# Convolution taps of two tiles moved into the next tile, and the head norm by a square root and a reciprocal

## The chip, the cores and the metric

One NeuronCore of one Trainium2 chip runs the kernel. The metric is the device time of one execution in microseconds, the median of several runs; before the change it is 1832.07 us (three runs, 1827.65 to 1835.13). TensorE does the matmuls, VectorE and ScalarE the elementwise work, GpSimd and SyncE issue DMAs.

## The reference

A decoder layer on 256 tokens of width 2048, in float32. What matters here is the first half:

```python
proj = x @ w_in                      # K, V, Q of two head groups, gates, u, gate_b, gate_c
o_att = _nsa(q, k_cmp, v_cmp, ...)   # 8 heads of 128, three branches each, softmax
y = gate_b * conv3(gate_c * u)       # depthwise, causal, width 3, 1024 channels
def _head_rmsnorm(y, g):             # over each of the 16 groups of 128
    yf = yf * rsqrt(mean(square(yf), -1) + 1e-6)
    return yf * g
mix = _head_rmsnorm(concatenate([o_att, o_conv]), head_norm_g)
h = layernorm(ALPHA * x + mix @ w_out)
```

Behind it stands the second half: queries and top-k over product keys, then for each token 128 gathered rows of `expert_u` (a dot product and a gelu) and 128 of `expert_v` (a weighted sum), and a last layer norm.

## The kernel before, in words

Each engine has its own instruction stream, written out by hand; streams meet only in semaphores, so the order of the Python calls of an engine is the order of its queue.

**Items.** The input projection is 22 tiles of 256 output columns; tile `t` has 8 items `(t, c)`, each two blocks of 128 rows of the weight. The output projection follows with items `O(j, i)`, `j` 0 to 3 and `i` 0 to 15. Each item's weight block (128x512) is split in two parts for a float32-like product: ScalarE writes the high part (`hi_to`, L839), VectorE the rest (`lo_to`, L1130), and TensorE multiplies (12 matmuls of 256 columns at L512 for an input item, 6 of 512 at L652 for an output item). The ring of split blocks has six slots, so ScalarE can be at most six items ahead of TensorE. `hi_to(end)` and `lo_to(end)` make the items before `end`; a step written under `(t, c)` of ScalarE or VectorE stands behind the split of item `(t, c-1)`.

**Tiles.** The kinds of tiles 12 to 21 are K V Q Q C U B C U B, and tiles 2 to 11 have the same order. Heads of group 0 are worked through in tiles 10 to 15, of group 1 in 16 to 21: `score` on TensorE at c = 6 of one tile (L599 to L605), in the next tile `bias` (VectorE, c = 1), `expo` (ScalarE, c = 2 to 4), `scale` (VectorE, c = 4), `transpose_probs` (TensorE, c = 4, L613), `probs_out` (both, c = 7), `attend` (TensorE, c = 6, L633) and `att_out` (ScalarE, in the tile after).

**Convolution.** A C tile leaves its result in `c_sb`. Behind a U tile VectorE makes the product (`conv_in`, L1198) and three taps (`conv_tap`, L1207 and L1209), each of two instructions and a drain, behind a B tile the output product (`conv_out`, L1216). `cu` and `cv` have one buffer each.

**Head norm.** For a pair of blocks: `square` (ScalarE), `mean_square` (TensorE with a matrix of ones, L640), `log_rms` and `inverse_rms` (ScalarE, Ln then Exp with scale -0.5, L918 and L921), `normed` (VectorE, two products, L1225). Then `mix_att` and `mix_conv` (ScalarE) make the high part of the activations, `lo_att` and `lo_conv` (VectorE, L1230 and L1236) the low part; the output projection takes these. Group 0 goes through these steps in tiles 16 and 17, group 1 in tile 21 and the items `O(0, i)`. `score` of group 1's first head waits for `rms_ok` 4, since the mean squares lie in its PSUM banks.

Where the norm of the second group stands in ScalarE's queue:

```python
                if (t, c) == (21, 6):
                    log_rms(0, 5)
                    log_rms(2, 6)
                if (t, c) == (21, 7):
                    log_rms(1, 7)
                    act.drain()
        hi_to(O(0, 0))
        inverse_rms(0)
        inverse_rms(2)
```

Of the kernel before, what the change touches and what calls it, by code (L numbers as in the profile page):

```python
# [14 lines left out]
SEQ = 256  # L15
# [59 lines left out]
def O(j, i):  # L75
    return ITEM["O", j, i]
# [18 lines left out]
def evicted(t):  # L95
    act_tiles = [i for i in range(TILES) if kind_of(i) in "KVQC"]
    dve_tiles = [i for i in range(TILES) if kind_of(i) in "cUB"]
    return ("acc_act", act_tiles.index(t) + 1) if t in act_tiles else ("acc_dve", dve_tiles.index(t) + 1)


def build(nc, x, w_in, cmp_k_pos, cmp_k_w1, cmp_k_b1, cmp_k_w2, cmp_v_pos, cmp_v_w1, cmp_v_b1, cmp_v_w2,
# [184 lines left out]
    def bview(i, *shape):  # L286
        n = 1
        for s in shape:
            n *= s
        names_ = "abc"[:len(shape)]  # L290
        if len(shape) == 1:
            return bank[i][:, 0:n]
        return bank[i][:, 0:n].rearrange("p (%s) -> p %s" % (" ".join(names_), " ".join(names_)),
                                         **dict(zip(names_, shape)))
# [196 lines left out]
    def _(pe):  # L491
# [177 lines left out]
        for t in range(2, TILES):  # L669
            sem, count = evicted(t - 2)  # L670
            pe.wait_ge(S[sem], count)
            for c in range(8):
                if t < 10:
                    c_slot(8 * (t - 2) + c)
                if (t, c) == (3, 4):
                    gate_logits()
                if (t, c) == (4, 4):
                    gate_transposes()
                if (t, c) == (6, 2):
                    hid_sum(0)  # L680
                if (t, c) == (10, 1):
                    hid_sum(1)
                if (t, c) == (10, 3):
                    hid_transposes()
                if (t, c) == (10, 5):
                    compressed()
                for g in range(NG):
                    r = t - 10 - 6 * g
                    if c == 4 and 1 <= r <= R:
                        transpose_probs(g, r - 1)  # L690
                    if c == 6 and 1 <= r <= R:
                        attend(g, r - 1)
                    if c == 6 and 0 <= r < R:
                        score(g, r)
                if (t, c) == (15, 6):
                    for n, ready in ((2, 1), (3, 2), (0, 3), (1, 4)):
                        mean_square(n, ready)
                if (t, c) == (21, 4):
                    mean_square(0, 5)
                    mean_square(2, 6)  # L700
                if (t, c) == (21, 5):
                    mean_square(1, 7)
                t_slot(t, c)

        for j in range(4):
            if j == 0:
                pe.wait_ge(S["y_att"], R * NG)
                pe.wait_ge(S["mix_ready"], 1)
            elif j == 1:
                for t in (20, 21):  # L710
                    pe.wait_ge(S[evicted(t)[0]], evicted(t)[1])
            else:
                pe.wait_ge(S["acc_dve"], 2 + 4 * NG + j - 1)
            if j == 3:
                pe.wait_ge(S["s_skeys"], 16)
                for n in range(4):
                    for i in range(4):
                        ins = nc.tensor.transpose(bank[2 + n][:, 128 * i:128 * i + 128], skeys[:, 4 * n + i, :], ident[:, :])
                    ins.then_inc(S["sk_mm"], 1)
            for i in range(KC):  # L720
                if (j, i) == (0, 5):
                    mean_square(3, 8)
                if (j, i) == (0, 8):
                    pe.wait_ge(S["mix_ready"], 2)
                if (j, i) == (0, 14):
                    pe.wait_ge(S["mix_ready"], 3)
                out_item(j, i)
# [92 lines left out]
    def _(act):  # L820
# [92 lines left out]
            nc.scalar.activation(sq[:, 2 * n:2 * n + 2, :], y_sb[:, 2 * n:2 * n + 2, :], ACT.Square  # L913
                                 ).then_inc(S["squared"], 1)

        def log_rms(n, count):
            act.wait_ge(S["norm_mm"], count)
            nc.scalar.activation(sq[:, 2 * n:2 * n + 2, :], bview(2 + n, 2, SEQ), ACT.Ln, bias=eps[:, 0:1])  # L918

        def inverse_rms(n):  # L920
            nc.scalar.activation(sq[:, 2 * n:2 * n + 2, :], sq[:, 2 * n:2 * n + 2, :], ACT.Exp, scale=-0.5  # L921
                                 ).then_inc(S["rms_ok"], 1)

        def mix_att(g):
# [19 lines left out]
        for t in range(2, TILES):  # L944
            for c in range(8):
# [30 lines left out]
                    square(0, 0)  # L976
                if (t, c) == (15, 2):
                    square(1, 0)
                if (t, c) == (16, 1):
                    log_rms(2, 1)  # L980
                    log_rms(3, 2)
                if (t, c) == (16, 2):
                    log_rms(0, 3)
                    log_rms(1, 4)
                    act.drain()
                if (t, c) == (16, 3):
                    for n in (2, 3):
                        inverse_rms(n)
                if (t, c) == (16, 4):
                    for n in (0, 1):  # L990
                        inverse_rms(n)
                if (t, c) == (16, 7):
                    mix_conv(0, 0, 4, 1)
                if (t, c) == (17, 0):
                    mix_att(0)
                if (t, c) == (20, 0):
                    square(0, 0)
# [1 line left out]
                    square(2, 3)  # L999
                if (t, c) == (21, 2):  # L1000
                    square(1, 0)
                if (t, c) == (21, 6):
                    log_rms(0, 5)
                    log_rms(2, 6)
                if (t, c) == (21, 7):
                    log_rms(1, 7)
                    act.drain()
        hi_to(O(0, 0))
        inverse_rms(0)
        inverse_rms(2)  # L1010
        hi_to(O(0, 1))
        inverse_rms(1)
        hi_to(O(0, 3))
        mix_att(1)
        hi_to(O(0, 4))
        mix_conv(1, 0, 2, 2)
        hi_to(O(0, 5))
        square(3, 4)
        hi_to(O(0, 9))
        log_rms(3, 8)  # L1020
        act.drain()
        hi_to(O(0, 10))
        inverse_rms(3)
        hi_to(O(0, 11))
        mix_conv(1, 2, 4, 3)
        for n in range(4):
            hi_to(O(3, 4 + n))
# [92 lines left out]
    def _(dve):  # L1120
# [80 lines left out]

        def conv_tap(t, tap):
            g, pair = (t - 2) // 10, (t - 2) % 10 // 8
            for b in range(2):
                w = params[:, 8 * tap + R * g + 2 * pair + b:8 * tap + R * g + 2 * pair + b + 1]
                if tap == 0:
                    V.tensor_scalar(cv[:, b, :], cu[:, b, 0:SEQ], w, None, ALU.mult)  # L1207
                else:
                    V.scalar_tensor_tensor(cv[:, b, :], cu[:, b, tap:tap + SEQ], w, cv[:, b, :], ALU.mult, ALU.add)  # L1209
            dve.drain()  # L1210
# [9 lines left out]
        def normed(g, n, count):  # L1220

            dve.wait_ge(S["rms_ok"], count)
            for b in range(2 * n, 2 * n + 2):
                col = 24 + NH * (b // 4) + R * g + b % 4
                V.scalar_tensor_tensor(y_sb[:, b, :], y_sb[:, b, :], params[:, col:col + 1], sq[:, b, :],  # L1225
                                       ALU.mult, ALU.mult)
# [43 lines left out]
        for t in range(2, TILES):  # L1270
            for c in range(8):
                lo_to(T(t, c))
                first = 2 if t < 10 else 5
                if t > 2 and c == first and kind_of(t - 1) == "U":
                    conv_in(t - 1)
                    conv_tap(t - 1, 0)
                if t > 2 and c == first + 1 and kind_of(t - 1) == "U":
                    conv_tap(t - 1, 1)
                if t > 2 and c == first + 2 and kind_of(t - 1) == "U":
                    conv_tap(t - 1, 2)  # L1280
                if t > 2 and c == first and kind_of(t - 1) == "B":
                    conv_out(t - 1)
                if (t, c) == (4, 6):
# [20 lines left out]
                for g in range(NG):  # L1304
# [4 lines left out]
                        scale(g, r)  # L1309
                    if 0 <= r < R and c == 7:  # L1310
                        probs_out(g, r)
                if (t, c) == (16, 4):
                    normed(0, 2, 1)
                if (t, c) == (16, 5):
                    normed(0, 3, 2)
                    dve.drain()
                if (t, c) == (16, 6):
                    normed(0, 0, 3)
                if (t, c) == (16, 7):
                    normed(0, 1, 4)  # L1320
                    dve.drain().then_inc(S["mixf_ready"], 1)
                if (t, c) == (17, 0):
                    lo_conv(0, 0, 4, 1)
                if (t, c) == (17, 3):
                    lo_att(0, 2)
                    dve.drain().then_inc(S["mix_ready"], 1)
        lo_to(O(0, 2))
        normed(1, 0, 5)
        normed(1, 2, 6)
        lo_to(O(0, 3))  # L1330
        normed(1, 1, 7)
        dve.drain().then_inc(S["mixf_ready"], 1)
        lo_to(O(0, 5))
        conv_out(21)
        lo_to(O(0, 6))
        lo_att(1, 3)
        lo_conv(1, 0, 2, 4)
        dve.drain().then_inc(S["mix_ready"], 1)
        lo_to(O(0, 10))
        normed(1, 3, 8)  # L1340
        dve.drain().then_inc(S["mixf_ready"], 1)
        lo_to(O(0, 12))
        lo_conv(1, 2, 4, 5)
        dve.drain().then_inc(S["mix_ready"], 1)
        for j in range(3):
# [197 lines left out]
```

## Time and profile before

| | |
|---|---|
| median of three runs | 1832.07 us (1827.65 to 1835.13) |
| the profiled execution | 1834.16 us, its span 1832.4 us |
| mean granted TensorE clock | 0.961 |
| TensorE busy | 1492.4 us, 81% of the span |
| VectorE busy | 1062.5 us, 58% |
| GpSimd busy | 754.5 us, 41% |
| ScalarE busy | 393.9 us, 21% |
| input and output projection | end at about 464 us |
| first expert gather | issued at 493.8 us |

The span is what lies between the first and the last instruction that the profile shows; the profiled execution's time is 1.8 us more. The busy shares are means over two stages: in the projections TensorE works almost without a pause, in the gathers the DMA engines do (421 GB/s from about 600 us on). A row of a timeline reads: start in us, duration in us, engine, line, instruction, output<-inputs, shape and count; in brackets stands the idle time of the engine ahead of it and what ended it.

### The profile page before, as it was taken

Reading aid. Unit: us, or ns where it says so; the run is one execution under the profiler, and the core shown is the slowest. Engines: PE = TensorE matmul, PEld = TensorE weight load, DVE = VectorE, ACT = ScalarE, POOL = GpSimd, SP = SyncE. Lnnn points to the kernel's source line nnn. Section 1 sums busy time; section 2 is a strip of 40 time slices with the busy share of each in tenths; the row PEclk is TensorE's granted clock in tenths of the full one; section 3 lists DMA queues with packets and bytes.
Section 4 is the critical chain, followed back from the end, with each engine's and each line's share of the span. In section 5 each row is a group of like instructions: output and inputs, shape, how many; then the busy total and the mean of one; then the engine's idle time right before and its main releaser. Section 6 shows DMA issues by size and latency. Waiting matters only on the chain.

```text
span 1832.4 us, 15277 instructions
## 1 busy us (share of the span) xinstructions
PE 1492.4 (81%) x5692; PEld 885.1 (48%) x5692; DVE 1062.5 (58%) x1696; ACT 393.9 (21%) x853; POOL 754.5 (41%) x591
## 2 busy tenths in 40 slices
PE   8999999999887428787787877777778788787896
PEld 7988998978876323333333333333333333233332
DVE  6665656565679997454545545454746454544434
ACT  5665464565101030101001011010110201010200
POOL 3210000000157768555455454555555555455341
PEclk9999999999998668999999999999999999999998
DMA  9885344376499999999999999999999999999995
GB/s 305 286 264 157 110 139 137 116 234 202 168 408 414 413 378 422 422 421 421 422 421 422 421 422 422 421 422 421 422 422 422 421 422 421 422 422 421 422 421 222
DMA packets 154043, 644.60 MB, mean 352 GB/s; under 512 B 11620, under 2 KB 64960, under 8 KB 87920
## 3 DMA queue, kind: packets, MB, share of 16 engines
q0 software_dynamic: 79376, 557.62, 74.0%
q1 hardware_dynamic: 74592, 85.99, 14.8%
q8 instruction: 45, 0.74, 0.2%
q14 instruction: 30, 0.25, 0.0%
HBM read 641.47 MB, written 2.10 MB: 351 GB/s over the span
## 4 chain that ended last, share of the span: by engine, by line
DMA 52%; PE 31%; POOL 6%; DVE 6%; issue 3%; DVEq 1%; ACT 1%; SPq 0%; POOLq 0%; ACTq 0%
DMA v_slot<-in_expert_v_dram,eid 50%; PE psum_all L512 12%; PE psum_all L813 7%; PE psum_all L652 4%; POOL u_slot L461 4%; DVE u_slot L1453 3%; PE psum_all L751 2%; POOL v_slot L476 2%; DMA u_slot<-in_expert_u_dram,eid 2%; PE psum_all L633 1%; PE psum_all L539 1%; PE psum_all L537 1%; DVE w_lo L1130 1%; PE psum_all L599 0%; ACT w_hi L839 0%
## 5 line engine op out<-in xcount | busy, mean ns | idle before, releaser
L813 PE MATMUL psum_all<-v_slot,diag 128*128 128x512 f32 x1968 | 906.0, 608 | 248.6 <-DMA v_slot<-in_expert_v_dram,eid 248.5
L1453 DVE SCALAR_TENSOR_TENSOR u_slot<-u_slot,xh 128x2048 f32<-128x2048 f32 x256 | 581.8, 2290 | 493.5 <-DMA u_slot<-in_expert_u_dram,eid 493.2
L813 PEld LDWEIGHTS psum_all<-v_slot,diag 128*128 128x128 f32 x1968 | 360.9, 191 | 793.1 <-issue 436.2
L476 POOL DMA_INDIRECT v_slot<-in_expert_v_dram,eid x256 | 349.4, 1365 | 463.5 <-PE psum_all L813 434.8
L461 POOL DMA_INDIRECT u_slot<-in_expert_u_dram,eid x256 | 367.8, 1437 | 219.6 <-DVE eid L1446 94.2
L1067 ACT ACTIVATE diag<-ident,gate 128x128 f32<-128x128 f32 x246 | 73.5, 388 | 710.7 <-PE psum_all L813 465.4
L1130 DVE TENSOR_TENSOR w_lo<-w_ring,w_hi 128x512 fp32r<-128x512 f32 x240 | 156.8, 687 | 87.9 <-ACT w_hi L839 85.0
L512 PE MATMUL psum_all<-act_hi,w_hi 128*128 128x256 f32 x640 | 186.5, 291 | 1.1 <-DVE w_lo L1130 1.0
L512 PE MATMUL psum_all<-act_hi,w_lo 128*128 128x256 f32 x640 | 181.8, 284 | 0.0
L512 PE MATMUL psum_all<-act_lo,w_hi 128*128 128x256 f32 x640 | 181.8, 284 | 0.0
L839 ACT ACTIVATE w_hi<-w_ring 128x512 fp32r<-128x512 f32 x240 | 139.3, 622 | 42.4 <-PE psum_all L512 40.6
L751 PE MATMUL psum_all<-hT,wq_ring 128*128 128x256 f32 (+1 forms) x576 | 122.1, 374 | 21.3 <-DMA wq_ring<-in_w_query_dram 20.8
L512 PEld LDWEIGHTS psum_all<-act_hi,w_hi 128*128 128x128 f32 x640 | 123.5, 193 | 13.6 <-issue 4.3
L512 PEld LDWEIGHTS psum_all<-act_lo,w_hi 128*128 128x128 f32 x640 | 123.3, 193 | 3.1 <-issue 0.7
L512 PEld LDWEIGHTS psum_all<-act_hi,w_lo 128*128 128x128 f32 x640 | 123.3, 193 | 0.0
L751 PEld LDWEIGHTS psum_all<-hT,wq_ring 128*128 128x128 f32 x576 | 104.7, 201 | 35.8 <-DMA wq_ring<-in_w_query_dram 22.3
L449 POOL DMA_DIRECT2D skeys<-in_sub_keys_dram x1 | 1.2, 1177 | 252.8 <-PE psum_all L652 252.8
L1058 ACT ACTIVATE u_act<-u_dot 128x16 f32<-128x16 f32 x16 | 3.4, 215 | 318.4 <-DVE u_slot L1453 318.4
L1130 DVE TENSOR_TENSOR w_lo<-wq_ring,w_hi 128x512 fp32r<-128x512 f32 x64 | 42.7, 690 | 28.0 <-ACT w_hi L839 27.7
L652 PE MATMUL psum_all<-w_hi,mix_hi 128*128 128x512 f32 x128 | 50.4, 394 | 3.5 <-DVE w_lo L1130 3.5
L1491 DVE SCALAR_TENSOR_TENSOR xh<-v_slot,gate,xh 128x2048 f32<-128x2048 f32 x10 | 23.5, 2351 | 51.0 <-DMA v_slot<-in_expert_v_dram,eid 51.0
L652 PE MATMUL psum_all<-w_hi,mix_lo 128*128 128x512 f32 x128 | 49.8, 389 | 0.0
(226 smaller groups left out, 1005.5 us busy)
## 6 DMA issues: line engine op xcount, KB each, us to landing
w_ring<-in_w_in_dram SPq DMA_DIRECT2D x88, 512.0 KB, 5.2
wq_ring<-in_w_out_dram SPq DMA_DIRECT2D x32, 512.0 KB, 5.0
wq_ring<-in_w_query_dram SPq DMA_DIRECT2D x32, 512.0 KB, 10.5
w_ring<-in_cmp_k_w_dram POOLq DMA_DIRECT2D x16, 512.0 KB, 6.5
w_ring<-in_cmp_v_w_dram POOLq DMA_DIRECT2D x16, 512.0 KB, 4.6
u_slot<-in_expert_u_dram,eid POOLq DMA_INDIRECT x256, 32.8
v_slot<-in_expert_v_dram,eid POOLq DMA_INDIRECT x256, 33.2
xh<-in_x_dram SPq DMA_DIRECT2D x4, 512.0 KB, 7.6
```

The source lines that it names most:

```text
L461: nc.gpsimd.indirect_dma_start(out=u_slot[m % RU][:, :], out_offset=None, in_=expert_u[0], in_offset=bass.IndirectOffsetOnAxis(ap=eid[:, n ...
L476: nc.gpsimd.indirect_dma_start(out=v_slot[m % RV][:, :], out_offset=None, in_=expert_v[0], in_offset=bass.IndirectOffsetOnAxis(ap=eid[:, n ...
L512: ins = nc.tensor.matmul(o, st, mv, start=(k == 0 and b == 0 and i == 0), stop=(k == KC - 1 and i == 2), skip_group_check=True)
L537: nc.tensor.matmul(acc[0:62, :], blk_hl[:, kv, j, 0:62], w_hi[:, n % RING, :], start=(j == 0), stop=False, skip_group_check=True)
L652: ins = nc.tensor.matmul(bank[acc + b][:, :], st[:, k, half], mv[:, n % RING, :], start=(i == 0 and m == 0), stop=(i == KC - 1 and m == 2))
L751: ins = nc.tensor.matmul(o, wq_ring[j % 2][:, k // 4, k % 4, 256 * (h % 2) + 128 * c:256 * (h % 2) + 128 * c + 128], hT[:, k, 128 * t0:128 ...
L813: ins = nc.tensor.matmul(bank[(4 if n < PH else 0) + q][:, :], diag[:, n % 2, k, :], v_slot[m % RV][:, 512 * q:512 * q + 512], start=m % ( ...
L839: nc.scalar.activation(w_hi[:, n % RING, :], raw_item(n), ACT.Copy).then_inc(S["hi_done"], 1)
L1067: ins = nc.scalar.activation(diag[:, n % 2, k, :], ident[:, :], ACT.Copy, scale=gate[:, n, k:k + 1])
L1130: V.tensor_tensor(w_lo[:, n % RING, :], raw_item(n), w_hi[:, n % RING, :].bitcast(F32), ALU.subtract).then_inc(S["lo_done"], 1)
L1453: V.scalar_tensor_tensor(u_slot[m % RU][:, :], u_slot[m % RU][:, :], 1.0, xh[:, n // PH, :], ALU.mult, ALU.mult, accum_out=u_dot[:, n, k:k ...
L1491: V.scalar_tensor_tensor(xh[:, 1, :], v_slot[m % RV][:, :], gate[:, n, k:k + 1], xh[:, 1, :], ALU.mult, ALU.add)
```

## The change

Three taps of tile 10 move from tile 11 (c = 5, 6, 7) to tile 12 (c = 0, 2, 3), those of tile 17 from tile 18 to tile 19 likewise; tiles 7 and 20 keep theirs. The root of the mean square is taken by Sqrt on ScalarE in one pass, its reciprocal on VectorE in `normed`, in place, with a drain. In tile 16 ScalarE has one root behind each of four items and VectorE one norm behind each of four; the steps that follow move by one to three items. In the second group no root is left in tile 21: the first three lie behind `O(0, 0)` and `O(0, 1)`, the mean squares all at (21, 5), the fourth ahead of `O(0, 7)` in place of `O(0, 5)`.

```diff
+TAP_AT = {7: ((8, 2), (8, 3), (8, 4)), 10: ((12, 0), (12, 2), (12, 3)), 17: ((19, 0), (19, 2), (19, 3)),
+          20: ((21, 5), (21, 6), (21, 7))}
...
-                if (t, c) == (21, 4):
+                if (t, c) == (21, 5):
                     mean_square(0, 5)
                     mean_square(2, 6)
-                if (t, c) == (21, 5):
                     mean_square(1, 7)
...
-                if (j, i) == (0, 5):
+                if (j, i) == (0, 7):
                     mean_square(3, 8)
...
-        def log_rms(n, count):
+        def root_rms(n, count):
             act.wait_ge(S["norm_mm"], count)
-            nc.scalar.activation(sq[:, 2 * n:2 * n + 2, :], bview(2 + n, 2, SEQ), ACT.Ln, bias=eps[:, 0:1])
-
-        def inverse_rms(n):
-            nc.scalar.activation(sq[:, 2 * n:2 * n + 2, :], sq[:, 2 * n:2 * n + 2, :], ACT.Exp, scale=-0.5
+            nc.scalar.activation(sq[:, 2 * n:2 * n + 2, :], bview(2 + n, 2, SEQ), ACT.Sqrt, bias=eps[:, 0:1]
                                  ).then_inc(S["rms_ok"], 1)
...
-                if (t, c) == (16, 1):
-                    log_rms(2, 1)
-                    log_rms(3, 2)
-                if (t, c) == (16, 2):
-                    log_rms(0, 3)
-                    log_rms(1, 4)
-                    act.drain()
-                if (t, c) == (16, 3):
-                    for n in (2, 3):
-                        inverse_rms(n)
-                if (t, c) == (16, 4):
-                    for n in (0, 1):
-                        inverse_rms(n)
-                if (t, c) == (16, 7):
+                if t == 16 and 1 <= c <= 4:
+                    root_rms((2, 3, 0, 1)[c - 1], c)
+                if (t, c) == (17, 0):
                     mix_conv(0, 0, 4, 1)
-                if (t, c) == (17, 0):
+                if (t, c) == (17, 1):
                     mix_att(0)
...
-                if (t, c) == (21, 6):
-                    log_rms(0, 5)
-                    log_rms(2, 6)
-                if (t, c) == (21, 7):
-                    log_rms(1, 7)
-                    act.drain()
-        hi_to(O(0, 0))
-        inverse_rms(0)
-        inverse_rms(2)
         hi_to(O(0, 1))
-        inverse_rms(1)
-        hi_to(O(0, 3))
+        root_rms(0, 5)
+        root_rms(2, 6)
+        hi_to(O(0, 2))
+        root_rms(1, 7)
+        hi_to(O(0, 6))
         mix_att(1)
-        hi_to(O(0, 4))
         mix_conv(1, 0, 2, 2)
-        hi_to(O(0, 5))
+        hi_to(O(0, 7))
         square(3, 4)
-        hi_to(O(0, 9))
-        log_rms(3, 8)
-        act.drain()
         hi_to(O(0, 10))
-        inverse_rms(3)
-        hi_to(O(0, 11))
+        root_rms(3, 8)
+        hi_to(O(0, 12))
         mix_conv(1, 2, 4, 3)
...
             g, pair = (t - 2) // 10, (t - 2) % 10 // 8
+            if tap == 0 and t in (10, 17):
+                dve.drain()
...
             dve.wait_ge(S["rms_ok"], count)
+            V.reciprocal(sq[:, 2 * n:2 * n + 2, :], sq[:, 2 * n:2 * n + 2, :])
+            dve.drain()
...
-                    conv_tap(t - 1, 0)
-                if t > 2 and c == first + 1 and kind_of(t - 1) == "U":
-                    conv_tap(t - 1, 1)
-                if t > 2 and c == first + 2 and kind_of(t - 1) == "U":
-                    conv_tap(t - 1, 2)
+                for u in (7, 10, 17, 20):
+                    for tap in range(3):
+                        if (t, c) == TAP_AT[u][tap]:
+                            conv_tap(u, tap)
...
-                if (t, c) == (16, 4):
-                    normed(0, 2, 1)
-                if (t, c) == (16, 5):
-                    normed(0, 3, 2)
-                    dve.drain()
-                if (t, c) == (16, 6):
-                    normed(0, 0, 3)
+                if t == 16 and 4 <= c <= 7:
+                    normed(0, (2, 3, 0, 1)[c - 4], c - 3)
                 if (t, c) == (16, 7):
-                    normed(0, 1, 4)
                     dve.drain().then_inc(S["mixf_ready"], 1)
-                if (t, c) == (17, 0):
+                if (t, c) == (17, 3):
                     lo_conv(0, 0, 4, 1)
-                if (t, c) == (17, 3):
+                if (t, c) == (17, 5):
                     lo_att(0, 2)
                     dve.drain().then_inc(S["mix_ready"], 1)
         lo_to(O(0, 2))
         normed(1, 0, 5)
+        lo_to(O(0, 3))
         normed(1, 2, 6)
-        lo_to(O(0, 3))
+        lo_to(O(0, 4))
         normed(1, 1, 7)
         dve.drain().then_inc(S["mixf_ready"], 1)
         lo_to(O(0, 5))
         conv_out(21)
-        lo_to(O(0, 6))
+        lo_to(O(0, 7))
         lo_att(1, 3)
+        lo_to(O(0, 8))
         lo_conv(1, 0, 2, 4)
         dve.drain().then_inc(S["mix_ready"], 1)
-        lo_to(O(0, 10))
+        lo_to(O(0, 11))
         normed(1, 3, 8)
         dve.drain().then_inc(S["mixf_ready"], 1)
-        lo_to(O(0, 12))
+        lo_to(O(0, 13))
         lo_conv(1, 2, 4, 5)
```

## Rows read from the trace of the kernel before

**Rows 1.** The page: the chain that ended last, by engine.
```profile
DMA 52%; PE 31%; POOL 6%; DVE 6%; issue 3%; DVEq 1%; ACT 1%; SPq 0%; POOLq 0%; ACTq 0%
```

**Rows 2.** Waits of TensorE, 0 to 430 us: total, times, longest.
```profile
PE psum_all L652 <- DVE w_lo L1130: 3.5, 4, 1.5
PE psum_all L633 <- DVE pTc L1191: 1.6, 1, 1.6
PE psum_all L633 <- issue: 1.5, 1, 1.5
```

**Rows 3.** VectorE's timeline, from 180 us.
```profile
182.97 0.75 DVE L1160 SCALAR_TENSOR_TENSOR sc<-dist,nslope,psum_all 128x512 f32<-128x512 f32 x1 [1.59 <-PE psum_all L605]
...
188.69 0.69 DVE L1130 TENSOR_TENSOR w_lo<-w_ring,w_hi 128x512 fp32r<-128x512 f32 x1 [0.60 <-ACT w_hi L839]
...
190.81 0.18 DVE L1184 TENSOR_TENSOR scc<-scc,rg 128x30 f32<-128x30 f32 x1
...
191.51 0.68 DVE L1198 TENSOR_TENSOR cu<-psum_all,c_sb 128x512 f32<-128x512 f32 x1
...
196.43 0.40 DVE L1191 COPY pTc<-psum_all 16x256 f32<-16x256 f32 x1
```

**Rows 4.** The chain that ended last, in order of time: start, duration, what.
```profile
196.98 3.51 PE psum_all L633 x16
...
204.01 9.31 PE psum_all L512 x72
...
233.76 2.36 PE psum_all L633 x16
...
237.98 8.73 PE psum_all L512 x72
...
250.46 2.36 PE psum_all L633 x16
...
313.28 3.73 PE psum_all L633 x16
...
320.53 9.11 PE psum_all L512 x72
...
361.27 1.72 PE psum_all L640 x4
...
383.08 57.42 PE psum_all L652 x252
```

**Rows 5.** A stretch of 4 us: busy times, granted clock, DMA share, GB/s.
```profile
198.00:202.00 4.00, 4.00 (x15) 3.28 (x15) 0.03 (x1) 0.90 (x2) 0.00 (x0) 0.55 0.89 238
```

**Rows 6.** Groups of VectorE instructions by form: busy, mean ns, idle before.
```profile
L1130 DVE TENSOR_TENSOR w_lo<-w_ring,w_hi 128x512 fp32r<-128x512 f32 x240 | 156.8, 687 | 87.9 <-ACT w_hi L839 85.0 <-issue 0.8
...
L1225 DVE SCALAR_TENSOR_TENSOR y_sb<-y_sb,params,sq 128x256 f32<-128x256 f32 x16 | 6.9, 480 | 1.2 <-ACT sq L921 1.2
...
L1459 DVE RECIPROCAL g_inv<-g_sum 128x1 f32<-128x1 f32 x16 | 2.5, 157 | 0.0
...
L1177 DVE RECIPROCAL rg<-sums 128x6 f32<-128x6 f32 x8 | 1.5, 183 | 0.0
...
L1180 DVE TENSOR_TENSOR rg<-rg,gates 128x6 f32<-128x6 f32 x8 | 1.3, 166 | 0.6
```

**Rows 7.** ScalarE's timeline, 255 to 365 us.
```profile
260.96 1.28 ACT L918 ACT_TABLE_LOAD   x1
265.43 0.69 ACT L918 ACTIVATE sq<-psum_all,eps 128x512 f32<-128x512 f32 x1 [3.18 <-PE psum_all L640]
...
285.18 0.51 ACT L884 ACTIVATE sc<-sc,nmx 128x256 f32<-128x256 f32 x1 [3.14 <-DVE nmx L1172]
...
362.17 0.69 ACT L918 ACTIVATE sq<-psum_all,eps 128x512 f32<-128x512 f32 x1 [4.69 <-PE psum_all L640]
```

**Rows 8.** TensorE's timeline, 276 to 292 us.
```profile
279.32 1.03 PE L599 MATMUL psum_all<-kT,qT 128*128 128x256 f32 x4
...
289.51 0.39 PE L512 MATMUL psum_all<-act_hi,w_hi 128*128 128x256 f32 x1 [0.26 <-DVE w_lo L1130]
```

## The prediction

> **What bounds the kernel now.** Read first the chain that ended last [rows 1]: DMA holds 52% of it and TensorE 31%. The DMA share is the expert gathers, which begin only after the input projection, the output projection, the layer norm and the first query scores. So the span is a TensorE stage of 464 us followed by gathers, and whatever the first stage saves reaches the end one for one, as long as nothing between waits for something other than the work before it; I found nothing of that kind. The change edits only the first stage, between 190 and 390 us.
>
> The waits of TensorE come next [rows 2]. It is busy nearly everywhere there: it waits 1.6 us once and 1.5 us once at L633 (the attention products of a head), and 3.5 us in four pieces at L652 (the output projection). These small waits are the prize, and with them what the clock does after them. The chain in order of time [rows 4] shows that. An undisturbed head starts L633 at 233.76 and its tile goes on at 237.98, 4.22 us later, and the next 72 matmuls take 8.73. After the first wait it is 196.98 to 204.01, 7.03 us, and then 9.31; after the second 313.28 to 320.53, 7.25, and then 9.11. In those microseconds the granted clock is 0.55 [rows 5], the lower of its levels (1.2 of 2.4 GHz) for most of the slice. TensorE had worked without a pause for 12 us before, then stood 1.6 us, then fell. So each wait costs itself and a second bill: 2.81 + 0.58 = 3.39 us for the first, 3.03 + 0.38 = 3.41 for the second.
>
> **Part A, the taps of tiles 10 and 17.** In the VectorE timeline [rows 3] the scaled probabilities of head 0 are out at 190.99. A split item, the gating product (191.51, 0.68), and then tap, item, tap, item, tap stand before the two copies that L633 waits for, which end at 196.83; L633 starts at 196.98, 1.6 us late. Moving the three taps takes them from between. The items stay: the product ends at 192.2, two items of 0.65 (0.687 long, but 0.62 apart in a row) [rows 6] bring 193.5, and the transposes are done by about 192.6, so the copies end at about 194.25. L633 can start when TensorE comes to it, at 196.98 - 1.6 = 195.4: a margin of 1.1 us. The same holds for tile 17.
>
> Where do the taps go? The first lands behind the copies, where VectorE stands idle until the next head's scores. The others go behind the second and third item of the next tile. Call S the moment a head's scores are out; in rows 3 that is 182.97, and the probabilities are out at S + 8.0. TensorE transposes them at S + 8.73 [rows 4] and comes to the next L633 at 250.46 - 237.98 = S + 12.48. In the wait for exponentials VectorE idles ahead of each of those items, 0.60 us ahead of the one at 188.69 and more ahead of the one before; a tap is 2 x 0.48 with some overlap, 0.87, plus a drain of 0.07. The second tap fits; the third overruns its gap by about 0.3. So the probabilities are out at S + 8.3 against S + 8.73, and the copies at about S + 11.85 against S + 12.48. Both margins hold, the smaller is 0.4. Part A gives 1.6 + 3.39 + 1.5 + 3.41 = **9.9 us**. Its bounds: 3.1, if the clock falls anyway, and 9.9, if not; I take 9.9, because the heads of rows 4 without a wait ran at full clock.
>
> **Part B, the norm of the first group (tile 16).** Removed on ScalarE: four Exp passes, and the table load between Ln and Exp. The Ln pass becomes a Sqrt of the same shape; I cost it like Ln, 0.69 [rows 7]. Added on VectorE: four reciprocals of 128x512 and four drains. Its price is the unknown. At small sizes the trace has it [rows 6]: 157 ns for one element, 183 for six, while an ordinary product of six takes 166. One of 512 takes about 0.69, a slope of (687 - 166) / 506 = 1.03 ns per element. The reciprocal's own slope from one to six is 26 / 5 = 5.2 ns, which drawn out to 512 would be 2.8 us; but most of it is the step that small operations show among themselves, and beside the product of six only 17 ns are left. So it lies between 0.53 (the slope alone) and 2.8, and I take 0.69, since it is nearest to the product.
>
> The first mean square is out at 265.4 [rows 7]. ScalarE runs Sqrt, item, Sqrt, item and is through the four at 269.4. VectorE finishes the third item at 269.5, and each norm is 0.69 + 0.07 + 0.88 and an item 0.65, 2.3 us: the norm of the four is complete at about 278.0. TensorE needs items (16,4) to (16,6) at 276.4, 277.9 and 281.2; they are there at 271.8, 274.1 and 276.4. Scores start at 279.32 [rows 8] and are out at S = 279.32 + (4.22 - 2.36) = 281.2. Before, the subtraction for the low parts of the convolution stands ahead of the head's bias. Now both subtractions are moved behind the third and fifth item, so the bias starts at S. The probabilities come at S + 8.5, TensorE is there at S + 8.73; the copies at S + 12.4 against S + 12.48. Nothing has room to spare, so I charge 0.3. Before, item (17,3) started at 289.51 where S + 5 x 1.455 = 288.45, 1.06 late, and there was some 0.3 more up to the head: 1.4. Part B gives 1.4 - 0.3 = **1.1 us**, with 0.69 for the reciprocal.
>
> A table load for Exp now stands ahead of the head's exponentials. ScalarE idled 3.14 us there [rows 7], by my times 2.8 after the change. In the trace a load runs ahead of the wait of its pass (Ln's in tile 16 ends 3.18 us before the pass can start, the idle time of that row), so its 1.28 are covered; without cover it would cost 1.3 once. The Trainium skill (ScalarE: Activation LUTs, "Table sets: the hidden batching unit" and "What ACT_TABLE_LOAD costs") speaks against mixing Exp and Sqrt, since they lie in different sets, and gives 2.66 us for a switch with its drain; the trace has 1.28 and starts the pass right behind. By the page's figure the load would still lie inside the idle time, by 0.1 us, and the sum would be the same.
>
> **Part C, the norm of the second group (tile 21 and the output projection).** From 361.27 to 383.08 [rows 4] TensorE does four mean squares (0.86 each), four items of tile 21 (1.455) and six of the projection (6 x 0.228 = 1.37): 3.44 + 5.82 + 8.2 = 17.46 of 21.81 us. So 4.35 us are lost. The reason is on ScalarE [rows 7]: it stands 4.69 us at the first Ln, with items (21,6) and (21,7) behind it in its queue, and VectorE stands behind those; then come two more Exp loads. After the change no norm step lies in tile 21. ScalarE makes (21,6), (21,7) and O(0,0) as slots come free, to 360.3, loads Sqrt while it waits, and is through three roots at 366.3. VectorE does tap 1 at about 359 as before, then (21,6), tap 2, (21,7), O(0,0) to 362.3, O(0,1) at 366.4, and norm, item, norm, item, norm to 372.5. TensorE wants O(0,0) at 369.6 and then one item each 1.37: O(0,2) at 372.4 (there at 368.7), O(0,3) at 373.7 (370.9), O(0,4) at 375.1 (373.2), O(0,5) at 376.4 (374.7), O(0,6) at 377.8 (375.4). The fourth mean square is moved behind that, its square is ready at 375.3; its root, norm and subtraction end at 386.2 and are wanted at 389.6. I find no wait left. Part C gives **4.3 us**; bounds: 4.35, all that is lost, and 2, taken lower than that delay would give, if the chain of norms on VectorE runs two microseconds later than I count, a little more than its least margin (1.7 at O(0,5)). The weight loads that the earlier splits release start earlier, on the one sync queue, and nothing waits on it here.
>
> Sum: 9.9 + 1.1 + 4.3 = 15.3 us, from 1834.16 of the profiled execution to 1818.9. That execution is 2.1 above the median, so in terms of the median 1832.07 - 15.3 = **1817**.
>
> **The rivals.**
> 1. The clock falls anyway, or one of the two waits stays (the taps' new places push the next head's copies past their 0.4 to 0.6 of margin). Two short waits gone without their clock give 3.1 + 1.1 + 4.3 = 8.5 us, 1823.5; one wait of two kept 15.3 - 4.9 = 10.4, 1821.7. Against it: three heads in a row without a wait and at full clock. Chance 0.13.
> 2. The reciprocal is dear, at the bound of 2.8 us. Each norm in tile 16 is 3.8, item (16,7) is out at 287.2 and the bias starts at 288.9, 7.7 behind S: 6.3 us lost against before (7.7 less the 1.4 lost there now), 9.7 if the clock falls there. In the projection O(0,3) and O(0,4) wait 1.6 and 3.1 and a later item 1.0, 1.5 us worse than before. Together -9.9 + 6.3 + 1.5 = -2.1, or +1.3: 1830 to 1833, no change. Chance 0.06.
> 3. The other side: the reciprocal works eight steps for each element, 8 x 1.03 x 512 = 4.2 us. Then the bias behind tile 16 starts at 295, 13.7 behind S (12.3 us lost against before, and 3.4 of clock) and the projection loses 7.3: -9.9 + 15.7 + 7.3 = +13, 1845. It ends slower by over 0.5% from about 3.9 us on. Six elements would then hold 49 of the 183 ns and one would take 142, not 157; that speaks against it. The Trainium skill (VectorE: DVE Perf Modes, "First, the fixed hardware budget") says the reciprocal is an iterative divide with a repeat count of 8, which could be read this way. Chance 0.04.
> 4. The saving is real but smaller, by new waits of 0.5 to 1 us in tile 17 or in O(0,2) to O(0,6), or is hidden by the scatter of the gathers (the three runs before span 7.5 us): 1820 to 1827. Chance 0.12.
>
> **How the numbers follow.** The forecast has 0.65, with 1813 to 1821 as its own range (Part C at 2 to 4.35, Part B at 0 to 1.4, scatter of 3). The range that leaves out 2 in 10 takes in rival 1 and most of 4: 1812 to 1825. About 0.5% (9 us, 1823) can be told from no change here. Faster: the forecast, half of rivals 1 and 4, 0.77; same: 0.18, with rival 2; slower: 0.05.
>
> **What would show it.** Part A: no idle time at L633 in tiles 11 and 18, and a granted clock of 1.00 where it was 0.55. Part B: RECIPROCAL 128x512 at about 0.69 us; the load of Exp ahead of the exponentials of tile 17 ended before them; L633 of tile 17 without a wait. Part C: O(0,0) to O(0,6) back to back, ScalarE's first root after O(0,0)'s split. The prediction is wrong if the reciprocal is over 1.5 us, if a new wait ahead of an L633 brings the clock down, or if the gathers' stage, 464 us to the end, changes its length.

## The result and the profile after

| | before | after |
|---|---|---|
| median | 1832.11 us (14 runs, 1826.39 to 1836.81) | 1838.28 us (14 runs, 1836.12 to 1839.22) |
| profiled execution | 1834.16, span 1832.4 | 1838.75, span 1836.8 |
| ratio, with 95% interval | | 1.0034 [1.0023, 1.0045] |

The kernel became 0.34% slower where 0.8% faster was forecast; the time lies 13 us above the upper end of the range. By the bound set in the prediction (0.5%) this is "no change", but the interval lies wholly above 1: the loss is small and real.

The first view to open is the one that the prediction staked itself on, VectorE's groups by form in the changed kernel (busy, mean ns of one, idle before):

```profile
L1204 DVE RECIPROCAL sq<-sq 128x512 f32<-128x512 f32 x8 | 26.8, 3346 | 0.0
L1437 DVE RECIPROCAL g_inv<-g_sum 128x1 f32<-128x1 f32 x16 | 2.5, 158 | 0.0
L1156 DVE RECIPROCAL rg<-sums 128x6 f32<-128x6 f32 x8 | 1.5, 184 | 0.0
```

A reciprocal of 128x512 takes 3.35 us, not 0.69. The short ones are as short as before [rows 6].

The waits of TensorE up to 430 us (total, times, longest) answer to [rows 2]:

```profile
PE psum_all L656 <- DVE w_lo L1109: 7.3, 3, 3.3
...
PE psum_all L516 <- DVE w_lo L1109: 6.6, 5, 3.1
```

Both waits at the attention products (now L637) are gone. In their place TensorE waits 6.6 us for splits of the input projection, in pieces of up to 3.1 and all but 0.5 of it in tiles 16 and 17, and 7.3 in the output projection, in pieces of up to 3.3. What holds the splits is plain in VectorE's timeline, tile 16 first, then the second group:

```profile
264.04 0.69 DVE L1109 TENSOR_TENSOR w_lo<-w_ring,w_hi 128x512 fp32r<-128x512 f32 x1 [0.41 <-ACT w_hi L842]
264.65 3.35 DVE L1204 RECIPROCAL sq<-sq 128x512 f32<-128x512 f32 x1
268.07 0.88 DVE L1208 SCALAR_TENSOR_TENSOR y_sb<-y_sb,params,sq 128x256 f32<-128x256 f32 x2
268.87 0.68 DVE L1109 TENSOR_TENSOR w_lo<-w_ring,w_hi 128x512 fp32r<-128x512 f32 x1
269.47 3.35 DVE L1204 RECIPROCAL sq<-sq 128x512 f32<-128x512 f32 x1
...
373.98 0.68 DVE L1109 TENSOR_TENSOR w_lo<-wq_ring,w_hi 128x512 fp32r<-128x512 f32 x1
374.58 3.35 DVE L1204 RECIPROCAL sq<-sq 128x512 f32<-128x512 f32 x1
378.00 0.88 DVE L1208 SCALAR_TENSOR_TENSOR y_sb<-y_sb,params,sq 128x256 f32<-128x256 f32 x2
379.00 0.69 DVE L1109 TENSOR_TENSOR w_lo<-wq_ring,w_hi 128x512 fp32r<-128x512 f32 x1
```

From 264.04 on each split comes 4.8 us after the last, while TensorE eats an item in 1.45. ScalarE's timeline shows the same from its side: it has filled the ring and stands until the norms are through, and the load of Exp has little idle time left to hide in:

```profile
283.48 1.06 ACT L930 ACTIVATE mix_hi<-y_sb 128x1024 fp32r<-128x1024 f32 x1 [13.91 <-DVEq L1297]
...
286.54 1.28 ACT L887 ACT_TABLE_LOAD   x1
288.45 0.51 ACT L887 ACTIVATE sc<-sc,nmx 128x256 f32<-128x256 f32 x1 [0.62 <-DVE nmx L1151]
...
378.95 1.06 ACT L926 ACTIVATE mix_hi<-y_sb 128x1024 fp32r<-128x1024 f32 x1 [10.06 <-DVEq L1309]
```

Windows of 4 us (busy time of PE, PEld, DVE, ACT, POOL; then granted clock, DMA share, GB/s) show the clock. The stretch of [rows 5] is now at 1.00, and the fall has moved to where the new waits are:

```profile
198.00:202.00 4.00, 4.00 (x32) 3.90 (x33) 2.11 (x5) 0.86 (x2) 0.00 (x0) 1.00 0.55 142
...
280.00:284.00 4.00, 1.15 (x8) 0.85 (x7) 3.81 (x4) 0.52 (x1) 0.00 (x0) 0.57 0.00 0
...
376.00:380.00 4.00, 0.72 (x3) 0.25 (x2) 3.81 (x5) 1.05 (x2) 0.00 (x0) 0.52 0.84 260
```

The chain in order of time (start, duration, what) gives the balance. These rows answer to [rows 4]:

```profile
195.56 2.36 PE psum_all L637 x16
...
199.78 8.73 PE psum_all L516 x72
...
259.72 0.87 PE psum_all L644 x2
...
294.28 0.56 PE psum_all L617 x4
...
361.34 1.73 PE psum_all L644 x4
...
393.56 50.62 PE psum_all L656 x222
...
467.76 0.69 DVE xh L1228
```

The last row starts where the output projection ends. The same marks in the trace of before are 264.53 (mean squares), 291.21 (transposes of tile 17), 361.27 (mean squares, one item of 1.455 us earlier in the order) and 464.07. So by stretches: to the mean squares 264.53 - 259.72 = 4.8 us gained (first taps); to tile 17, 34.56 against 26.68, 7.9 lost (norm of the first group); to tile 21, 65.6 against 70.1, 4.5 gained (second taps); to the end, 107.9 against 102.8, 5.1 lost (norm of the second group). Together 3.7 us lost, 467.76 - 464.07. The gathers' stage is 0.7 us longer in this trace than in that of before (1365.1 against 1364.4), so the spans differ by 4.4. The medians differ by 6.2; the section on why the prediction was wrong tells where the rest is.

### The profile page after: what moved, and what is told of

It reads as the page before. It is cut to its first block, busy times and chain, and to the rows that moved or that the text cites. A ratio compares the mean times of both kernels' runs of the same rounds, so it can differ in the third digit from the quotient of the medians.

```text
span 1836.8 us, 15279 instructions
## 1 busy us (share of the span) xinstructions
PE 1492.0 (81%) x5692; PEld 883.5 (48%) x5692; DVE 1088.9 (59%) x1704; ACT 384.2 (21%) x841; POOL 754.6 (41%) x591
## 4 chain that ended last, share of the span: by engine, by line
DMA 53%; PE 31%; DVE 6%; POOL 5%; issue 2%; DVEq 1%; ACT 1%; SPq 0%; POOLq 0%
DMA v_slot<-in_expert_v_dram,eid 50%; PE psum_all L516 13%; PE psum_all L816 7%; PE psum_all L656 4%; POOL u_slot L465 4%; DVE u_slot L1431 3%; PE psum_all L754 2%; DMA u_slot<-in_expert_u_dram,eid 2%; POOL v_slot L480 1%; PE psum_all L637 1%; DVE sq L1204 1%; PE psum_all L543 1%; PE psum_all L541 1%; DVEq L1205 1%; DVE w_lo L1109 1%
## 6 DMA issues: line engine op xcount, KB each, us to landing
wq_ring<-in_w_query_dram SPq DMA_DIRECT2D x32, 512.0 KB, 18.8
```

## The experiments

The kernel before was run again beside each set of experiments, and its medians differ between the three sets: 1832.1 beside the changed kernel, 1827.9 beside experiments 1 to 4, 1833.8 beside 5 to 7. A ratio is always to the runs of before in the same set, and each experiment is also read by its own trace. Experiments 3 and 5 leave the reciprocal out of some norms, so their results are wrong and only their times are used.

**1. The taps alone.** Edit: the diff's lines of `TAP_AT`, the drain and the loop over it, on the kernel before.

```diff
+TAP_AT = {7: ((8, 2), (8, 3), (8, 4)), 10: ((12, 0), (12, 2), (12, 3)), 17: ((19, 0), (19, 2), (19, 3)),
...
+                        if (t, c) == TAP_AT[u][tap]:
+                            conv_tap(u, tap)
```

> The kernel before with the three taps of tiles 10 and 17 moved and nothing else. Theory (each short wait at the attention products costs itself and 3.4 us at the lower clock, and the moved taps end both): 9.9 us faster than before, no idle time of TensorE at that line, granted clock 1.00 behind it. Rival (the clock falls there whatever stands before it): 3.1 us faster.

Measured: 1825.52 us (12 runs, 1823.81 to 1826.6), ratio 0.9978 [0.9966, 0.9989], so 4 us by the ratio, 2.4 by the medians. The waits at the attention products are gone and the clock is 1.00 behind them:

```profile
198.00:202.00 4.00, 4.00 (x33) 3.92 (x32) 2.31 (x6) 0.66 (x2) 0.00 (x0) 1.00 0.47 119
```

Its trace reaches the first normalised `xh` at 458.07 us against 467.98 in the profiled execution of before: 9.9 us, the forecast to the tenth. Its median gives less than half. Neither theory as written fits both. The two numbers look to be about different executions of the kernel before; experiments 2 and 6 bear on this.

**2. The norm alone.** Edit: the changed kernel with the taps back, and without the drain that went with them.

```diff
-TAP_AT = {7: ((8, 2), (8, 3), (8, 4)), 10: ((12, 0), (12, 2), (12, 3)), 17: ((19, 0), (19, 2), (19, 3)),
+TAP_AT = {7: ((8, 2), (8, 3), (8, 4)), 10: ((11, 5), (11, 6), (11, 7)), 17: ((18, 5), (18, 6), (18, 7)),
...
-            if tap == 0 and t in (10, 17):
-                dve.drain()
```

> The changed kernel with the taps back in their old places, so the norm part alone. Theory (two parts of opposite sign: the taps give 9.9 us, the norm with its dear reciprocal takes them and some 6 more): about 16 us slower than before, 0.9%. Rival (the taps gave little, the norm costs only what is seen): 6 us slower.

Measured: 1844.16 us (6 runs), ratio 1.0074 [1.0052, 1.0096]; 16.3 us by the medians, 13.5 by the ratio. So the norm part alone loses 13 to 16 us, as the first theory has it, and the taps take some of it back. The front stage of its trace is only 9.8 us longer than that of before (first normalised `xh` at 477.73 against 467.98), and the trace shows why. Both waits at the attention products are there, 1.6 and 1.5 us long, yet only the first is followed by a fall of the clock. The chain in tile 18, behind the second wait:

```profile
321.21 2.60 PE psum_all L637 x16
...
325.67 8.74 PE psum_all L516 x72
```

and the windows of the stretch behind each wait:

```profile
320.00:324.00 4.00, 2.79 (x17) 2.34 (x18) 2.24 (x5) 0.15 (x1) 0.00 (x0) 1.00 0.27 62
...
200.00:204.00 4.00, 4.00 (x15) 3.42 (x15) 0.00 (x0) 0.90 (x2) 0.00 (x0) 0.50 0.60 156
```

From 321.21 to 325.67 are 4.46 us, where an undisturbed head has 4.22. In the trace of before the same wait of 1.5 us at the same place is followed by 7.25 us. The same wait has two prices, some 0.2 and 3.4 us. The norm's 7.9 + 5.1 = 13.0 us, less one fall of 3.4 that did not come, are 9.6, near the 9.8 of the trace.

**3. A product in the reciprocal's place.** Edit, on the changed kernel:

```diff
-            V.reciprocal(sq[:, 2 * n:2 * n + 2, :], sq[:, 2 * n:2 * n + 2, :])
+            V.tensor_tensor(sq[:, 2 * n:2 * n + 2, :], sq[:, 2 * n:2 * n + 2, :], sq[:, 2 * n:2 * n + 2, :], ALU.mult)
```

> The changed kernel, all steps in the same places, but each of the eight reciprocals of 128x512 is a product of the same size (so the norm uses the square of the root, not its reciprocal). Theory (the only step of the prediction that failed is the duration of the reciprocal, 0.69 taken and 3.35 measured): the product takes 0.69 us and the kernel 15 us less than before, about 1817. Rival (the Sqrt pass, the load of Exp ahead of tile 17 or the new order cost as well): no faster than about 1825.

Measured: 1818.85 us (6 runs), ratio 0.9941 [0.9919, 0.9962]; the eight products take 0.684 us each. No wait for a split is left in tiles 16 and 17 or in the projection, and the chain runs through both groups:

```profile
288.47 2.36 PE psum_all L637 x16
...
351.40 2.57 PE psum_all L644 x6
...
358.28 9.55 PE psum_all L656 x42
...
368.70 55.80 PE psum_all L656 x246
```

The x42 are seven output items back to back, the mean square of the fourth pair, then the rest without a gap. The projection ends at 448.06, 16.0 us before that of before (464.07). This is the kernel that the prediction reckoned with, at 1834.16 - 15.3 = 1818.9. By the stretches used above, the trace gains 5.5 us up to the mean squares and 4.5 from tile 17 to tile 21 (Part A: 9.9 forecast), 1.35 from the mean squares to tile 17 (Part B: 1.1) and 4.7 behind (Part C: 4.3). With the reciprocal at a product's price, every term comes out within 0.4 us. That the median meets 1818.9 so closely is in part luck: the profiled execution of this kernel took 1817.84.

**4. The disputed cost by itself.** Edit, on the changed kernel behind VectorE's last step:

```diff
+        for m in (1, 2, 4, 8, 16, 32, 64, 128, 256, 512):
+            dve.drain()
+            V.reciprocal(u_slot[0][:, 0:m], ln2g_sb[:, 0:m])
+            dve.drain()
+            V.tensor_tensor(u_slot[1][:, 0:m], ln2g_sb[:, 0:m], ln2g_sb[:, 0:m], ALU.mult)
```

> The changed kernel with pairs of a reciprocal and a product of 1, 2, 4, ... 512 columns behind its last step on VectorE. Theory A (a constant price for each column, (3346 - 184) / 506 = 6.25 ns, from the first column on): 128x64 takes about 0.55 us, 128x256 about 1.75, and between 1 and 8 columns the growth is 44 ns. Theory B (short ones run at the pace of a product and a slower pace sets in with size): 128x16 and 128x32 within 20 ns of the product. The same reciprocal on 32 partitions tells whether the partitions matter: 3.35 us if not.

The kernel was run once (1853.23 us, with the added work at its end), and only the durations in its trace are used. VectorE's timeline behind the last step:

```profile
1834.85 0.16 DVE L1498 RECIPROCAL u_slot<-ln2g_sb 128x1 f32<-128x1 f32 x1
...
1836.28 0.20 DVE L1498 RECIPROCAL u_slot<-ln2g_sb 128x8 f32<-128x8 f32 x1
1836.56 0.17 DVE L1500 TENSOR_TENSOR u_slot<-ln2g_sb 128x8 f32<-128x8 f32 x1
...
1837.37 0.35 DVE L1498 RECIPROCAL u_slot<-ln2g_sb 128x32 f32<-128x32 f32 x1
1837.80 0.19 DVE L1500 TENSOR_TENSOR u_slot<-ln2g_sb 128x32 f32<-128x32 f32 x1
...
1838.07 0.55 DVE L1498 RECIPROCAL u_slot<-ln2g_sb 128x64 f32<-128x64 f32 x1
...
1840.39 1.75 DVE L1498 RECIPROCAL u_slot<-ln2g_sb 128x256 f32<-128x256 f32 x1
...
1842.71 3.35 DVE L1498 RECIPROCAL u_slot<-ln2g_sb 128x512 f32<-128x512 f32 x1
1846.14 0.69 DVE L1500 TENSOR_TENSOR u_slot<-ln2g_sb 128x512 f32<-128x512 f32 x1
1846.90 3.34 DVE L1502 RECIPROCAL u_slot<-ln2g_sb 32x512 f32<-32x512 f32 x1
```

Theory A holds from the first columns on: (3.35 - 0.55) / 448 = 6.25 ns per column, against (0.69 - 0.19) / 480 = 1.04 for the product, six times as much. A quarter of the partitions takes as long (3.34 us). At 128x32 the two are already 0.16 us apart, which rules out theory B.

**5. Where the reciprocals hurt.** Edit, on the changed kernel:

```diff
+            if g == 0:
+                V.reciprocal(sq[:, 2 * n:2 * n + 2, :], sq[:, 2 * n:2 * n + 2, :])
+            else:
+                V.tensor_tensor(sq[:, 2 * n:2 * n + 2, :], sq[:, 2 * n:2 * n + 2, :], sq[:, 2 * n:2 * n + 2, :], ALU.mult)
```

> The changed kernel with its reciprocals in the first group's norm alone and a product of the same size in the second. From the two traces the first group's reciprocals cost 7.9 + 1.1 = 9.0 us against the product and the second group's 5.1 + 4.3 = 9.4. Theory (two separate costs that add): about 9 us above the kernel with the product in both, so 1828. Rival (the second is late because the first was): less than 4 us below the changed kernel.

Measured: 1828.40 us (12 runs, 1827.62 to 1829.09), 9.6 above the kernel with eight products and 9.9 below the changed kernel. The rival, which had less than 4 us below the changed kernel, is out. The trace says the same by stretches: from the mean squares to tile 17 it has 34.55 us, as the changed kernel (34.56; 25.33 with eight products), and from tile 21 to the end 98.1, as with eight products (98.1; 107.9 in the changed kernel). So the two costs, 9.2 and 9.8 us, are separate and add.

**6. The clock behind a wait.** Edit, on the kernel before: the three taps of tiles 10 and 17 are done twice, so that each of the two waits is longer.

```diff
                     conv_tap(t - 1, 2)
+                    if t in (11, 18):
+                        for tap in range(3):
+                            conv_tap(t - 1, tap)
```

> The kernel before, but the three taps of tiles 10 and 17 are done twice in a row (same result), so that each of the two waits at the attention products is some 2.6 us longer. Theory (after a wait of 1.6 us the clock falls in some executions and not in others, which is why the runs of before lie in three heaps, near 1827.5, 1831.5 and 1835; after one of 4 us it falls in every one): one heap, near 1827.5 + 5.2 + 6.8 = 1839.5, with a span of the runs under 4 us. Rival (the heaps come from the gathers): the same three heaps, each 5.2 us or more higher.

Measured: 1841.59 us (6 runs, 1840.40 to 1843.12), one heap with a span of 2.7 us, and 2.1 us above the 1839.5 expected. The waits are 4.2 and 4.1 us, and the clock falls with both (granted 0.50 at 200 to 204 us and at 320 to 324). The chain:

```profile
199.01 4.64 PE psum_all L633 x16
...
207.18 8.80 PE psum_all L512 x72
...
318.57 4.64 PE psum_all L633 x16
...
326.73 8.76 PE psum_all L512 x72
```

From 199.01 to 207.18 it is 8.17 us against 4.22. The 16 products take 4.64 us, about twice the 2.36 of an undisturbed head (3.51 in [rows 4]), so they run at the lower clock nearly from the first on, and a fall costs 4.0 us in place of 3.4. The lowest heap plus 2 x 2.6 plus 2 x 4.0 is 1840.7, near what was measured.

The 48 runs of before lie at 1825.6 to 1828.8 (20 runs), 1830.8 to 1832.4 (12) and 1833.8 to 1836.8 (16). The middles of these heaps, 1827.6, 1831.6 and 1835.2, are 3.7 to 4.0 us apart, about a fall each. Their mix differs between the sets, which is why the medians do: 4, 6 and 4 runs beside the changed kernel, 12, 2 and 3 beside experiments 1 to 4, and 4, 4 and 9 beside 5 to 7. That the heaps are executions with no, one and two falls is inferred, not shown: there is one trace of the kernel before, from the top heap, and it has both falls. Three things speak for it. The same wait has two prices in experiment 2. The mean granted clock, recorded for 34 of these runs, is 0.968 in the lowest heap, 0.964 in the middle one and 0.963 in the top one; it sets the lowest apart and hardly parts the other two. And the rival, that the heaps come from the gathers, has the traces against it: from the first normalised `xh` to the end of the span it is 1832.4 - 467.98 = 1364.4 us before, 1365.1 after, 1365.2 with the taps alone, 1364.7 with the norm alone and 1364.6 here, a spread smaller than the gap between two heaps. Since they are single traces of different kernels, they do not exclude it.

**7. Ln and Exp in the new places.** The changed kernel, its steps set apart as in the change, but without the reciprocal:

```diff
+        def inverse_rms(n):
+            nc.scalar.activation(sq[:, 2 * n:2 * n + 2, :], sq[:, 2 * n:2 * n + 2, :], ACT.Exp, scale=-0.5
+                                 ).then_inc(S["rms_ok"], 1)
...
+                if (t, c) == (16, 5):
+                    act.drain()
+                    inverse_rms(2)
+                    inverse_rms(3)
+                if (t, c) == (16, 6):
+                    inverse_rms(0)
+                    inverse_rms(1)
...
         root_rms(1, 7)
+        act.drain()
+        for n in (0, 2, 1):
+            inverse_rms(n)
...
         hi_to(O(0, 12))
+        act.drain()
+        inverse_rms(3)
...
-            V.reciprocal(sq[:, 2 * n:2 * n + 2, :], sq[:, 2 * n:2 * n + 2, :])
-            dve.drain()
```

(`root_rms` does Ln here; VectorE does two norms at (16, 6) and two at (16, 7).)

> The changed kernel (taps moved, the norm's steps and the steps behind it in the new places) with Ln and Exp on ScalarE in place of Sqrt and reciprocal: in tile 16 one Ln behind each of four items, two Exp at (16,5) and two at (16,6), in the second group the Exp passes behind the third Ln and, for the last pair, behind O(0,11). Theory (only the reciprocal's 3.35 us hurt; ScalarE has the room): no wait left but at most 1 us in the projection, front stage within 1 us of that with the product, so 1818 to 1821, faster than both kernels. Rival (the table loads between Ln and Exp hold the splits again): 1822 or more.

Measured: 1819.34 us (6 runs, 1818.71 to 1821.08), ratio 0.9934 [0.9914, 0.9954], within the 1818 to 1821 expected. It beats both kernels, with the four Exp passes of each group and the table loads kept. TensorE waits nowhere between its first input and the layer norm for more than 0.5 us:

```profile
PE psum_all L742 <- DVE xh L1372: 4.9, 1, 4.9
...
PE psum_all L516 <- DVE w_lo L1124: 0.5, 1, 0.5
```

So the new order was what paid. The Exp passes and loads that the change removed cost next to nothing once the steps stand apart: only for the fourth pair of the second group do a load (369.69, 1.28 us) and an Exp pass stand in the chain, and there TensorE is held up by some 0.2 us.

## Why the prediction was wrong, point by point

**The step that failed** is in Part B: "So it lies between 0.53 (the slope alone) and 2.8, and I take 0.69, since it is nearest to the product." It measured 3.35, above the upper bound. So the norm of the first group, for which Part B forecast a gain of 1.1 us, lost 7.9, and that of the second, for which Part C forecast a gain of 4.3, lost 5.1. The rows gave the slope, 26 / 5 = 5.2 ns for a column, and experiment 4 measured 6.25. I argued this slope away as a step that small operations share, by comparing a reciprocal and a product of six columns, where 17 ns of difference seemed little. By experiment 4 the reciprocal costs 6.25 - 1.04 = 5.2 ns a column more than the product, 31 ns on six columns, and the fixed parts of the two need not be equal. Where a slope of the operation itself is in the trace, it outweighs a likeness to another operation. The bound of 2.8 was that slope drawn out over 511 columns plus the 157 ns of the first, and left the slope no error. It was short by 1.05 ns on each column, 0.54 us in all. A slope taken from five columns and two different lines is too rough for that, and its end should not have been a wall.

**The rivals** had it between them. Rival 2 (2.8 us) said -2.1 or +1.3, rival 3 (4.2 us) +13; at 3.35 it was +4.6 by the profiled executions (1838.75 - 1834.16). Interpolated between +1.3 and +13 that would be 6, so the mechanism of both, norms that hold splits until TensorE starves and its clock falls, was the right one, and its price nearly so. They had 0.10 of the chance. The rule of the Trainium skill named beside rival 3 (VectorE: DVE Perf Modes, "First, the fixed hardware budget": an iterative divide with a repeat count of 8) did point to the side that came true; the trace's price is 6.25 / 1.04, six of a product's columns and not eight. I gave it 0.04 because "one would take 142, not 157". That speaks against eight steps and not against six: at 6.25 ns a column the 183 ns of six columns put one column at 152. I weighed 2.8 and 4.2 and no price between them.

**Part A** (9.9 us): near the forecast in the traces (4.8 and 4.5 in the changed kernel, 9.9 in the taps alone). The margins held: the new head in tile 19 was late by 0.2 us, that of tile 12 not at all. But 9.9 was read from a profiled execution in which the clock fell behind both waits. If the heaps are what experiment 6 takes them for, it fell about once in a median execution beside the changed kernel, so the taps are worth 6.5 there, and 3.1 in the lowest heap. Against the lowest heap of its own set (mean 1827.6) the kernel with the taps moved gained 2.3; the 0.8 that is missing is within what the gathers' stage varies by.

**Part B** other than the reciprocal: right. The four roots took 260.61 to 264.59, the Exp load was covered (it ended 0.62 us before its pass could start), and with the product no wait was left but the 0.3 us charged ahead of tile 17's head (284.40 to 288.47, 4.07 us against 3.75). **Part C** (4.3 us): right with the product, 4.4 over the stretch that it added up (23.2 us in [rows 4] with one more output item, 18.8 here).

**From the profiled execution to the median** was the second error. The prediction took the difference of 2.1 us off and called 1817; the kernel with the product measured 1818.85, which is 1834.16 less 15.3. The savings belonged to that execution, in the top heap; counted against its own time they come out, counted against the median they were too large. For the forecast this was the small error of the two. It explains also why the medians differ by 6.2 us where the traces differ by 4.4: before was profiled above its median (2.1), after only 0.5 above.

**The gathers' stage** kept its length as forecast: 1363.8 to 1365.5 us in the eight traces that end with it.

## What to carry to other kernels

Price an operation at the size at which it will run; if the trace has it only small, draw its own slope out to that size and give the bound that nobody wants a real chance, above all when the whole change stands on an engine that feeds the busy one. When the runs of a kernel lie in heaps, find out in which heap the profile was taken before a saving read from it is subtracted from a median. And separate what a change moves from what it replaces: here the moving was worth 12 us by the ratio of experiment 7 (15 from the profiled execution of before), and the replacement cost 19.

## What the runs showed of the hardware that I had not expected

A reciprocal on VectorE takes 6.25 ns for each column from the first on (3.35 us for 128x512, 3.34 for 32x512), six times a product's 1.04. A wait of TensorE of 1.5 or 1.6 us between two stretches of full work is sometimes followed by 3.4 us of loss at the lower clock and sometimes not: experiment 2 has both in one execution, and in the changed kernel TensorE waits 1.2 and 1.5 us for splits between 272 and 280 us, and 2.4 between 372 and 376, with the granted clock at 1.00 in those slices; the clock is at 0.57 and 0.52 only in the slices of the 3.1 and the 3.3 us wait. The waits of 4.1 and 4.2 us in experiment 6 cost 4.0 more each. What decides about a short wait stays open. That one short wait makes a kernel's time come in two values would follow, and removing two did narrow the spread of the runs: 1826.2 to 1835.9 for before and 1823.8 to 1826.6 with the taps moved, in the same set.
